# The modulation's partition sums: ones as the stationary side on four groups of array columns, columns made by transposes one product later

## The reference, cut to what matters

```
cond = silu(c)                                  # 1024 values
mod = cond @ w_ada[l] + b_ada[l]                # w_ada 1024 x 6144
sh1, sc1, g1, sh2, sc2, g2 = split(mod, 6)      # 1024 each
h = rms_norm(x, norm_mix_g) * (1 + sc1) + sh1   # before the third layer's projection
x = x + g1 * mix
h = rms_norm(x, norm_ffn_g) * (1 + sc2) + sh2   # before its feed-forward part
x = x + g2 * ffn
```

## Time and profile before

| what | value |
|---|---|
| median of three runs | 1954.52 us (1953.22 to 1956.26) |
| profiled execution: time, span of the core | 1952.16 us, 1950.4 us |
| TensorE busy | 1873.7 us, 96% |
| TensorE weight loads busy | 1516.8 us, 78% |
| VectorE busy | 1188.0 us, 61% |
| ScalarE busy | 732.4 us, 38% |
| GpSimd busy | 138.8 us, 7% |
| DMA | 184.06 MB, mean 94 GB/s |
| mean granted clock of TensorE | 0.983 |

### The profile page before, as it was taken

The page is one execution under the profiler, slowest core; times in us unless marked ns, Lnnn a source line. Parts: engine busy times, 40 slices in busy tenths (PEclk is TensorE's granted clock), DMA queues, the critical chain, the costliest instruction groups (busy, mean ns, idle before and its releaser), DMA issues.

```text
span 1950.4 us, 23146 instructions
## 1 busy us (share of the span) xinstructions
PE 1873.7 (96%) x9232; PEld 1516.8 (78%) x9232; DVE 1188.0 (61%) x2191; ACT 732.4 (38%) x1143; POOL 138.8 (7%) x136
## 2 busy tenths in 40 slices
PE   9989999999999999999999999889899799999997
PEld 7765788888888888788888888667566688888885
DVE  4999676545556686577454555866775554334338
ACT  4447352222233434545222223435554352222221
POOL 0343000000000152000000000000130000000000
PEclk9999999999999999999999999999999899999999
DMA  6220425433442121133433343021000503333221
GB/s 203 65 65 2 151 87 172 152 130 134 147 147 72 65 65 60 55 123 120 139 115 123 108 137 102 23 90 62 1 1 33 173 26 105 97 98 101 93 87 44
DMA packets 116876, 184.06 MB, mean 94 GB/s; under 512 B 7153, under 2 KB 71793, under 8 KB 113697
## 3 DMA queue, kind: packets, MB, share of 16 engines
q1 hardware_dynamic: 115376, 177.77, 27.5%
q0 software_dynamic: 1392, 4.82, 0.8%
HBM read 180.47 MB, written 2.10 MB: 94 GB/s over the span
## 4 chain that ended last, share of the span: by engine, by line
PE 75%; DVE 16%; ACT 5%; issue 3%; POOL 1%; DMA 0%; DVEq 0%; ACTq 0%
PE bank L592 10%; PE bank L593 10%; PE bank L594 10%; PE bank L770 7%; PE bank L771 7%; PE bank L769 7%; PE bank L566 2%; PE bank L568 2%; PE bank L567 2%; DVE wl L1833 2%; DVE gb L2186 2%; DVE m L2184 1%; PE bank L614 1%; PE bank L616 1%; PE bank L615 1%
## 5 line engine op out<-in xcount | busy, mean ns | idle before, releaser
L1833 DVE TENSOR_TENSOR wl<-raw,wh 128x2048 fp32r<-128x2048 f32 (+1 forms) x138 | 310.7, 2257 | 195.0 <-ACT wh L1226 194.7
L1226 ACT ACTIVATE wh<-raw 128x2048 fp32r<-128x2048 f32 (+1 forms) x142 | 265.1, 1883 | 250.0 <-PE bank L771 89.8
L592 PE MATMUL bank<-xh,wh 128*128 128x512 f32 (+2 forms) x880 | 346.6, 394 | 2.2 <-DVE wl L1833 2.2
L593 PE MATMUL bank<-xh,wl 128*128 128x512 f32 (+2 forms) x880 | 346.1, 393 | 0.0
L594 PE MATMUL bank<-xl,wh 128*128 128x512 f32 (+2 forms) x880 | 345.9, 393 | 0.0
L771 PE MATMUL bank<-wh,ul 128*128 128x512 f32 x592 | 230.4, 389 | 0.0
L770 PE MATMUL bank<-wl,uh 128*128 128x512 f32 x592 | 230.4, 389 | 0.0
L769 PE MATMUL bank<-wh,uh 128*128 128x512 f32 x592 | 230.4, 389 | 0.0
L592 PEld LDWEIGHTS bank<-xh,wh 128*128 128x128 f32 (+2 forms) x880 | 164.6, 187 | 41.9 <-DVE wl L1833 3.1
L594 PEld LDWEIGHTS bank<-xl,wh 128*128 128x128 f32 (+2 forms) x880 | 164.6, 187 | 38.5
L593 PEld LDWEIGHTS bank<-xh,wl 128*128 128x128 f32 (+2 forms) x880 | 164.5, 187 | 37.9
(11 more groups left out here) (361 smaller groups left out, 3123.7 us busy)
## 6 DMA issues: line engine op xcount, KB each, us to landing
raw<-in_mlp_w_up SPq DMA_DIRECT2D x32, 1024.0 KB, 5.6
raw<-in_mlp_w_down SPq DMA_DIRECT2D x32, 1024.0 KB, 5.1
raw<-in_w_ada SPq DMA_DIRECT2D x24, 1024.0 KB, 4.9
raw<-in_b_w_in SPq DMA_DIRECT2D x12, 1024.0 KB, 5.2
raw<-in_w_in SPq DMA_DIRECT2D x11, 1024.0 KB, 5.2
raw<-in_w_gate SPq DMA_DIRECT2D x11, 1024.0 KB, 5.4
raw<-in_w_up SPq DMA_DIRECT2D x11, 1024.0 KB, 5.3
raw<-in_w_down SPq DMA_DIRECT2D x10, 1024.0 KB, 5.0
```

What stands on the lines that cost most here:

```text
L592: pe.matmul(o, H[:, k, c], xh[:, k, :], start=k == 0, stop=False)
L593: pe.matmul(o, L[:, k, c], xh[:, k, :], start=False, stop=False)
L1226: act.activation(slots[slot_of[i]][0][:, 0:n], raw[:, i % NRAW, 0:n], ACT.Copy).then_inc(*s_high.up(i))
L1833: dve.tensor_tensor(L[:, 0:n], raw[:, i % NRAW, 0:n], H[:, 0:n].bitcast(F), ALU.subtract).then_inc(*s_low.up(i))
```

## The change

TensorE's ada_sum now uses ones, 128x32, as the stationary side and a quarter of acc, 128x512, as the moving side: four products for each r, product g writing the partitions 32g to 32g+31 of one bank. All 32 partitions of a group hold the same row of 512 sums. ScalarE copies the bank to ada_rows in A (ada_copy, 128x512). TensorE turns the four 128x128 pieces of ada_rows into a second bank (ada_turn, four transposes), and VectorE reads one column in 32 from it for the two adds (ada_sum).

Places: ada_turn stands behind the next up product (in mlp), behind row(0) (in cross), and behind the first panel_row (in m2). On ScalarE the copy stands behind first_half of down, and at the two ends of the MLPs behind the conversions ahead. On VectorE ada_sum no longer stands at the end of down but behind the next up product, behind scale(t), or behind last_row(0); CS1 is made before last_row(0), CS2 after ada_sum.

```diff
+        ada_rows = A[:, 12288:12800]
...
 # tensor_program
-            jobs = []
+            jobs, summed = [], []
...
                 row(0)
+                ada_turn()
                 row(1)
...
             def ada_sum():
                 while cur.owed:
                     r = cur.owed.pop()
                     b = banks.take(("ada", r))
                     w.wait_ge(*banks.free(("ada", r), s_act.sem))
                     w.wait_ge(*s_low.at(("ada", r)))
-                    for j in range(16):
-                        step = pe.matmul(bank[b][:, j:j + 1], acc[:, j * P:(j + 1) * P], ones[:, 0:1], start=True, stop=True)
+                    for g in range(4):
+                        step = pe.matmul(bank[b][32 * g:32 * g + 32, :], ones[:, 0:32], acc[:, g * 512:(g + 1) * 512], start=True, stop=True)
                     step.then_inc(*s_mm.up(("ada", r)))
+                    summed.append(r)
+
+            def ada_turn():
+
+                while summed:
+                    r = summed.pop()
+                    b = banks.take(("adaT", r))
+                    w.wait_ge(*banks.free(("adaT", r), s_act.sem))
+                    w.wait_ge(*s_act.at(("ada", r)))
+                    for j in range(4):
+                        step = pe.transpose(bank[b][:, j * P:(j + 1) * P], ada_rows[:, j * P:(j + 1) * P], ident)
+                    step.then_inc(*s_turn.up(("adaT", r)))
...
                     for q in range(2):
                         gemm_T((key, "up", n, q), x_key)
+                        ada_turn()
                     down(key, n - 1, 4, False, look if n == 7 else 1)
...
                 panel_row(("m2", "down", 7), uh[:, 1], ul[:, 1], 0, lambda f: s_xlow.at(("m2", "u", 7)), 4, True, i, t)
+                ada_turn()
...
 # scalar_program
             def cross(x_key, gain, shift, n_groups):
                 cur.take(high, n_groups + 1)
                 cur.take(high, 0)
+                ada_copy()
...
                     first_half(look if n == 7 else 1)
-                cur.owed.clear()
+                    if n < 7:
+                        ada_copy()
+
+            def ada_copy():
+                while cur.owed:
+                    r = cur.owed.pop()
+                    w.wait_ge(*s_mm.at(("ada", r)))
+                    copy_to(("ada", r), ada_rows, bank[banks.of["ada", r]][:, :])
...
             cur.take(high, 3)
             cur.take(high, 0)
+            ada_copy()
...
 # vector_program
                     scale(t)
+                    ada_sum()
...
             def ada_sum():
-                while cur.owed:
-                    r = cur.owed.pop()
-                    w.wait_ge(*s_mm.at(("ada", r)))
+                while summed:
+                    r = summed.pop()
+                    w.wait_ge(*s_turn.at(("adaT", r)))
+                    sums = bank[banks.of.get(("adaT", r), 0)][:, :].rearrange("p (j g r) -> p g j r", j=4, g=4)
                     for q in range(2):
-                        bc = BADA[:, 16 * r + 8 * q:16 * r + 8 * q + 8]
-                        dve.tensor_tensor(mod_cols[2 * r + q], bank[banks.of["ada", r]][:, 8 * q:8 * q + 8], bc,
-                                          ALU.add).then_inc(*s_step.up(("mod", r)))
-                    banks.read["ada", r] = s_step.at(("mod", r))
+                        m, bc = (v.rearrange("p (g j) -> p g j", j=4)
+                                 for v in (mod_cols[2 * r + q], BADA[:, 16 * r + 8 * q:16 * r + 8 * q + 8]))
+                        dve.tensor_tensor(m, sums[:, 2 * q:2 * q + 2, :, 0], bc, ALU.add).then_inc(*s_step.up(("mod", r)))
+                    banks.read["adaT", r] = s_step.at(("mod", r))
...
                         gemm_T((key, "up", n, q), evict_later)
+                        ada_sum()
...
-                    ada_sum()
+                    summed.extend(cur.owed)
+                    cur.owed.clear()
...
-            w.wait_ge(*s_step.at(("mod", 2)))
+            w.wait_ge(*s_step.at(("mod", 0)))
             dve.tensor_scalar(CS1, SC1, 1.0, None, ALU.add).then_inc(*s_step.up())
             w.wait_ge(*s_step.now())
             dve.tensor_tensor(CS1, CS1, GM, ALU.mult).then_inc(*s_step.up("cs1"))
+            last_row(0)
+            ada_sum()
+            w.wait_ge(*s_step.at(("mod", 2)))
             dve.tensor_scalar(CS2, SC2, 1.0, None, ALU.add).then_inc(*s_step.up())
             w.wait_ge(*s_step.now())
             dve.tensor_tensor(CS2, CS2, GF, ALU.mult).then_inc(*s_step.up("cs2"))
-            last_row(0)
             last_row(1)
```

## The result

| | median | runs |
|---|---|---|
| before | 1953.87 us | 6, 1950.65 to 1960.14 |
| after | 1942.01 us | 6, 1940.71 to 1947.47 |

The ratio is 0.994, with an interval of 0.9927 to 0.9953: 11.9 us less, where 10.1 were forecast, and 1942.0 us where 1944.4 were. In two further comparisons (1955.07 and 1955.58 us before) the changed kernel had 1943.29 and 1942.23 us, the ratio 0.9941 both times. The profiled execution of the changed kernel is the slowest of its six, 1947.47 us around a span of 1945.5; why is read further down.

What follows compares the result with a forecast made beforehand. The chain that ended last ran 75% through TensorE and 16% through VectorE. Gains of 1.79, 4.97 and 3.3 us at the three calls, 10.1 us, taken from the 1954.52 us median, gave 1944.4 us, range 1940.5 to 1950.

Steps and rivals of the forecast that it cites:

- The passes of the old call: TensorE, three old ada_sum calls: 32 one-column passes of 0.109 us each, 3.58 us a call, 10.7 us together.
- The new sum: TensorE, each new ada_sum: four products overlapping in four column groups, mode changes included, 1.30 us a call.
- The turn: TensorE, four 128x128 transposes a round: 0.40 us plus 0.09 for the product behind, 0.49 us.
- The covers: ScalarE's copy ends before the turn is due: 6, 3.8 and 4 us to spare in the three rounds, so no wait.
- VectorE's chain: Third round: without its 2.78 us wait for the sum, VectorE makes its low parts earlier; end 3.3 us earlier.
- The clock: TensorE behind the second and third old calls: half clock costs 4.8 us; the new calls keep full clock.
- more comes back: Case: an execution that also lost the clock at the first call (3.2 us) gains that too: 1941 us, chance 0.05.
- Behind 1240 nothing is touched: Stages after 1240 us in the timeline: unchanged by the edit, they only start earlier.
- The clock falls all the same: Rival, behind the new sums: half clock stays, 4.8 us of gain lost, 1949.2 us; chance 0.12.
- Pairs only: Rival, new sum: only two groups overlap, 2.1 us a sum, 2.4 us more in all, 1946.8 us; chance 0.10.
- one after another: Rival, new sum: four groups without overlap, 4.25 us a round, gain 2.7 us, 1951.8 us; chance 0.07.
- Every pass drained: Rival, new sum: each group's pass alone, 6.1 us a round, 2.8 to 7.6 us slower; chance 0.04.

Runs made afterwards that it cites:

- the turn right behind the sum: Changed kernel with ada_turn directly behind ada_sum in down, not one product further on: median 1949.39 us, ratio 0.9971.

## Why the prediction was right, step by step

- **The passes of the old call, 10.7 us in three.** Right: 3.68, 3.59, 3.62 wherever the clock stays up, 10.9 in all. The 60 cycles of the page, by which the change would have lost about 1 us a call, were rightly put aside: 109 ns a pass in every form of the old call, whether 1, 32 or 128 columns move. The Trainium skill has the better rule in another place (TensorE: Matmul & The Clock Gate, LDWEIGHTS): a weight load takes its columns over 1.2, in ns, an estimate of 107 ns for 128, and with this the passes agree.
- **The new sum, 1.30 us.** 1.19. The overlap read off two groups in the earlier trace rows held for four, and the groups start closer than there: within 0.03 us all four, where 3 x 0.04 = 0.12 was taken. Changing to groups took 0.08 us from the due time to the first pass (408.86 to 408.94), where 0.14 was taken; changing back about 0.20, where 0.18 was.
- **The turn, 0.49 us.** 0.44, from the earlier trace rows.
- **The covers.** The copy ended at 410.68, 590.07 and 1203.62, the turns came at 421.24, 593.93 and 1207.68: 10.6, 3.9 and 4.1 us of cover for the turn. In the first round the chunk queued behind the copy was the tighter one, as the prediction had it. The changed kernel there, ScalarE and VectorE:

```profile
410.08 0.60 ACT L1343 ACTIVATE A<-bank 128x512 f32<-128x512 f32 x1 [17.21 <-PE bank L753]
410.57 1.92 ACT L1243 ACTIVATE wh<-raw 128x2048 fp32r<-128x2048 f32 x1
412.59 2.29 DVE L1859 TENSOR_TENSOR wl<-raw,wh 128x2048 fp32r<-128x2048 f32 x1 [1.16 <-ACT wh L1243]
```

The low part ends at 414.88 (415 was worked out), and the first product that can want it starts at 421.60, behind the turn: 6.7 us, where 6 were said. Without the turn's cover, as the turn right behind the sum showed, the kernel loses 7.2 us.
- **VectorE's chain, 3.3 us.** 3.5 from the profile of the earlier trace rows to the changed one (32.90 to 29.41), with the wait for xl the same, 2.98; against the other two profiles of the kernel before (34.50), which lose more clock at this call, it is 5.1. The order in which VectorE does its small adds gave 1.9 of it at that place.
- **The clock, 4.8 us.** The mechanism was right: the calls make it fall, the new ones do not. The size was read from one execution. In the earlier trace rows two calls lose 4.7 to 4.8 us; in the other two profiles of the same kernel it was 6.3 and 7.9, and the profile that the sum stood on was 2.4 us under the median of its runs. The prediction added these 2.4 back as if they belonged to work that stays. By the spread of the falls, some of it was clock lost at these calls in the median execution, and the change removed that too. This is the mis-sized term: three profile pairs give 10.7, 13.9 and 12.3 us on TensorE, 11.9 were measured between the medians, 10.1 were forecast. It had a chance of 0.05 as a case that "more comes back", named for the first call only; 7 falls in 9 calls would have justified more. That this is the cause of the 1.8 us is not shown: the medians themselves spread nearly as much (1953.87 to 1955.58 before, 1942.01 to 1943.29 after), and so does the rest of the program.
- **"Behind 1240 nothing is touched", and what lies between the calls.** The prediction let every microsecond gained at the second call arrive at the third. In two of three profiles of the changed kernel 1.8 and 2.6 us of it were lost again behind L938. The forecast's nearness to the result owes something to luck here: the clock came back more at the calls than was taken, and some of it was lost elsewhere.
- **The rivals.** "The clock falls all the same": 0 falls in 9 rounds of the changed kernel, and none in 3 with a stationary side of 32 columns working alone for 3.5 us. "Pairs only" would have been 1.87 us for the sum, "one after another" 3.55: the experiments with two and one group show what they would have looked like, and at what price (1949.3 and 1952.2; the prediction had 1946.8 and 1951.8). At the calls the pairs cost 2.6 us more than four groups, close to the 2.4 forecast; the rest of their 6.1 lies elsewhere. "Every pass drained" did not happen in any form.

## What to carry to other kernels

A float32 matmul whose result is a column pays in this kernel what its 128-column stationary side costs, however few columns move: 109 ns a pass. If the small operand (ones, a vector) goes to the stationary side and the products are put on separate groups of array columns, four of them take about the time of one (1.00 us for four, 0.86 for the passes of one); the price is a transpose of the result, which costs TensorE little only where other products stand between sum and turn while another engine makes the copy. And where the clock's falls are part of the sum, read several executions: a profile gives the passes exactly and the falls by luck. Look at the clock in the later stages too: in two of three executions here, one fall less at a call stood beside one more further on.

## What the runs showed of the hardware beyond what was expected

- A float32 pass with a 128x128 stationary side takes 109 ns with 1, 32 and 128 moving columns alike. Weight loads are listed with 108, 136 and about 190 ns for 32, 64 and 128 columns.
- Four groups of 32 columns: four 512-column float32 products in 1.00 us, against 1.87 in two groups and 3.55 in one; the four first passes start within 0.03 us. From the ordinary product ahead, changing to groups took 0.08 us more than a usual step. Changing back took about 0.20: the last group's pass starts at 409.42 and needs 0.43, the next product starts at 409.94, 0.09 later, and its successor is 0.11 late.
- The clock: at the end of 3.5 us of one-column products or behind them it fell to 1.2 GHz in 7 of 9 calls; behind 128-column ones of the same length in 0 of 6; behind 3.5 us of 512-column products that use 32 of the array's 128 columns in 0 of 3. What the engine did before these falls was to move few columns, not to fill few columns of the array. Filling few rows is another matter: eight passes of 512 columns with 16 of 128 rows filled (3.6 us at full clock) had a fall in or behind them in 6 of 14 profiles. What the falls cost varied too (1.5 or 3.2 us at the calls).
- The Trainium skill (TensorE: Matmul & The Clock Gate, Part 4) says that transposes do not count as busy for the clock in the same way. Behind the changed kernel's nine turns of four transposes, 0.36 us each between full products, no fall was seen; no run here has a longer stretch of them at these places.
- An idle of 1.84 us ahead of four transposes was followed by half clock, one of 1.64 and one of 0.81 in the same execution were not.
